# Prompt attention of a hybrid encoder step: the two maps of a differential head joined before the values product

## The reference

```python
logits = jnp.einsum('bqhcd,blhcd->bhcql', qb, kb).astype(f32) * (DH_B ** -0.5)
logits = logits - _alibi_slopes(H_B)[None, :, None, None, None] * dist
logits = jnp.where(adm, logits, -jnp.inf)
p = jax.nn.softmax(logits, axis=-1)
a = (p[:, :, 0] - lam * p[:, :, 1]).astype(vb.dtype)
return jnp.einsum('bhql,blhe->bqhe', a, vb)
```

## Time and profile before

| | us |
|---|---|
| median of 3 runs | 4177.35 (4172.96 to 4182.59) |
| the profiled execution | 4171.43 |
| its span, first to last instruction | 4169.9 |
| prompt attention in it, first logits to last output | 1378.2 |
| mean granted TensorE clock | 0.94 |

### The profile page before, as it was taken

How to read it: one execution, slowest core, us unless ns; L and a number is a source line. 1 busy time by engine, 2 the same in 40 slices (tenths; PEclk the granted TensorE clock), 3 DMA queues, 4 the chain that set the end, 5 groups by cost and what they waited for, 6 DMA issues and landing times. The chain is left out here.

```text
span 4169.9 us, 56226 instructions
## 1 busy us (share of the span) xinstructions
PE 3748.4 (90%) x20713; PEld 3178.6 (76%) x20713; DVE 2326.8 (56%) x4784; ACT 1676.0 (40%) x2562; POOL 186.8 (4%) x373
## 2 busy tenths in 40 slices
PE   8989996884788988888988799999999999989997
PEld 6877883443677878888987678877888788779996
DVE  4335651444788888888775344445445444544334
ACT  2223431112566767777875422232323232322221
POOL 0001110000000000000000010001000100010000
PEclk9999995996799999999999899999999999999998
DMA  5556435627322121111100132223223322322121
GB/s 156 156 153 207 158 131 170 201 69 194 74 50 55 40 51 35 35 36 37 26 16 16 52 131 86 105 101 131 101 101 111 111 102 99 126 96 80 61 79 46
DMA packets 279876, 394.51 MB, mean 95 GB/s; under 512 B 29584, under 2 KB 181136, under 8 KB 270864
## 3 DMA queue, kind: packets, MB, share of 16 engines
q1 hardware_dynamic: 244208, 336.77, 25.9%
q0 software_dynamic: 12160, 44.18, 3.3%
q10 hardware_dynamic: 23328, 11.22, 1.1%
HBM read 320.32 MB, written 71.80 MB: 94 GB/s over the span
## 5 line engine op out<-in xcount | busy, mean ns | idle before, releaser
L1138 PE MATMUL pPV<-pV,pPTr 128*128 128x128 f32 (+1 forms) x4864 | 651.4, 282 | 36.8 <-ACT pPTr L1202 21.4
L1138 PEld LDWEIGHTS pPV<-pV,pPTr 128*128 128x128 f32 x4864 | 613.8, 198 | 57.6 <-issue 15.7
L1202 ACT ACTIVATE pPTr<-pTP 128x512 f32<-128x512 f32 (+3 forms) x704 | 355.7, 535 | 284.2 <-PE pTP L1125 281.5
L2167 ACT ACTIVATE fRU<-fUP 128x512 f32<-128x512 f32 (+1 forms) x128 | 80.0, 625 | 930.6 <-PE fUP L2037 930.6
L2037 PE MATMUL fUP<-fA_hi,fW_hi 128*128 128x512 f32 (+1 forms) x1280 | 418.9, 360 | 20.0 <-DVE fA_lo L2209 20.0
L2037 PE MATMUL fDN<-fW_hi,fU_hi 128*128 128x512 f32 x1088 | 423.6, 389 | 2.1 <-DVE fY L2307 2.1
L2037 PE MATMUL fDN<-fW_lo,fU_hi 128*128 128x512 f32 x1088 | 423.4, 389 | 0.0
L2037 PE MATMUL fDN<-fW_hi,fU_lo 128*128 128x512 f32 x1088 | 423.2, 389 | 0.0
L2037 PE MATMUL fUP<-fA_lo,fW_hi 128*128 128x512 f32 (+1 forms) x1280 | 418.3, 359 | 0.0
L2037 PE MATMUL fUP<-fA_hi,fW_lo 128*128 128x512 f32 (+1 forms) x1280 | 417.8, 359 | 0.0
L2203 DVE TENSOR_TENSOR fW_lo<-fW_raw,fW_hi 128x2048 fp32r<-128x2048 f32 x144 | 333.3, 2336 | 129.6 <-ACT fW_hi L2122 129.6
(11 more groups left out here) (237 smaller groups left out, 6254.2 us busy)
## 6 DMA issues: line engine op xcount, KB each, us to landing
fW_raw<-w_up SPq DMA_DIRECT2D x64, 1024.0 KB, 5.0
fW_raw<-w_down SPq DMA_DIRECT2D x64, 1024.0 KB, 4.9
qT<-qOUT SPq DMA_DIRECT2D x40, 512.0 KB, 3.3
sKB<-cache_kb SPq DMA_DIRECT2D x8, 2048.0 KB, 14.0
sVB<-cache_vb SPq DMA_DIRECT2D x8, 2048.0 KB, 8.4
pQA<-qT SPq DMA_DIRECT2D x64, 256.0 KB, 4.9
pQB<-qT SPq DMA_DIRECT2D x64, 256.0 KB, 5.0
fW_raw<-w_o SPq DMA_DIRECT2D x16, 1024.0 KB, 5.5
```

The costliest lines, as they stand in the source:

```text
L1138: mm = pe.matmul(PV[g % 2][:, 0:size], PTr[n % 3][:, j - 4 * k, :], V[:, j, a:a + size], start=(j == 0), stop=(j == blk[t] - 1))
L1202: act.activation(PTr[n % 3][:, 0:size, :], TP[bank_use[("p", n)] % 2][:, 0:size, :], ACT.Copy).then_inc(s_pt, 1)
L2167: act.activation(RU[:, 0:nt * P].rearrange("p (n w) -> p n w", n=n), UP[f % 2][:, 0:n, 0:width], ACT.Relu).then_inc(s_ru, 1)
```

## The change

The two maps of a B head are joined before the values. When both rows of exp are there, DVE computes a coefficient c = sum0 * (-lambda) / sum1 and, in one pass over the n keys, X1 = X1 * c + X0. Only the joined row, that of the odd job, is transposed and multiplied with V; its output is scaled with 1/sum0. So each head has one apply instead of two, and OM's and the lambda product's small steps go.

Around it: X has three buffers; PE makes logits three jobs ahead, the first half early in a job and the rest late; ACT's exp runs two jobs ahead; DVE's round g takes the pass of job g + 2, and inverts two sums at once in every even round. The fused pass multiplies by -slope and takes the minimum, so that the minimum itself is the bias of exp (scale -1), and the bias product goes. The selection is laid out anew: one ACT count in every job 0 to 12, five DVE steps in each of the rounds 1 to 12, and all that remains (two small steps and the mask passes) in round 13, where before it was spread up to round 15. The lambdas are loaded into OT's memory, and a third X buffer is zeroed at the start.

```diff
+    XB, AHEAD = 3, 3
+    def applied(g):
+        return g % JOBS < H_A or g % 2 == 1
...
             def select_steps(m):
-            last = count(HALVINGS)
+            last = HALVINGS // 2
             if m == 0:
-                return (0, 0), (0, 0)
...
+                return 0, 1
+            if m <= last:
+                return count(2 * m - 2) + 1, count(2 * m)
+            if m == last + 1:
+                return count(2 * m - 2) + 1, SEL
+            return SEL, SEL
...
         def _(pe):
-                early = g + 2 < NG and groups[t] > 1
+                early = g + AHEAD < NG and groups[t] > 1
                 transposes(0)
                 for k in range(1, groups[t]):
                     transposes(k)
                     if k == 1 and early:
-                        queries_keys(g + 2, slice(0, 2))
+                        logits(g + AHEAD, slice(0, 1))
                     products(k - 1)
-                if g + 2 < NG:
-                    queries_keys(g + 2, slice(2, None) if early else slice(None))
+                if g + AHEAD < NG:
+                    logits(g + AHEAD, slice(1, None) if early else slice(None))
                 products(groups[t] - 1)
...
-                apply(g)
+                if applied(g):
+                    apply(g)
+                elif g + AHEAD < NG:
+                    logits(g + AHEAD)
...
         def _(act):
             def softmax(g):
-                act.wait_ge(s_nm, g + 1)
-                act.activation(X[g % 2][:, 0:n_of[t]], X[g % 2][:, 0:n_of[t]], ACT.Exp,
-                               bias=nm[:, g % 2:g % 2 + 1], scale=slope,
+                act.wait_ge(s_lx, halves_before(g + 1))
...
+                act.activation(X[g % XB][:, 0:n_of[t]], X[g % XB][:, 0:n_of[t]], ACT.Exp,
+                               bias=mx[:, g % 4, k:k + 1], scale=-1.0,
...
-                for k in range(groups[t]):
-                    if k == 2 and g + 1 < NG:
-                        softmax(g + 1)
+                for k in range(groups[t] if applied(g) else 0):
+                    if k == 2 and g + 2 < NG:
+                        softmax(g + 2)
...
         def _(dve):
-                if g >= 2:
-                    dve.wait_ge(s_tr, groups_before(g - 1))
+                if g >= XB:
+                    if applied(g - XB):
+                        dve.wait_ge(s_tr, groups_before(g - XB + 1))
+                    else:
+                        dve.wait_ge(s_cb, combined_before(g - XB + 1))
...
-                                             scale=1.0, scalar=mx[:, i, k - 1:k] if k else -3.0e38,
-                                             op0=ALU.add, op1=ALU.max, accum_out=mx[:, i, k:k + 1])\
+                                             scale=-SLOPE[m], scalar=mx[:, i, k - 1:k] if k else 3.0e38,
+                                             op0=ALU.add, op1=ALU.min, accum_out=mx[:, i, k:k + 1])\
...
+            def combine(g):
+                n = n_of[g // JOBS]
+                i, j = g % 4, combined_before(g)
+                c = cf[:, j % 2:j % 2 + 1]
+                dve.wait_ge(s_ri, g // 2 + 1)
+                dve.tensor_scalar(c, sm[:, i:i + 1], lv[:, 5:6], ri[:, i + 1:i + 2], ALU.mult, ALU.mult)\
+                    .then_inc(s_cf, 1)
+                dve.wait_ge(s_cf, j + 1)
+                x = X[(g + 1) % XB][:, 0:n]
+                dve.scalar_tensor_tensor(x, x, c, X[g % XB][:, 0:n], ALU.mult, ALU.add).then_inc(s_cb, 1)
...
             for g in range(NG):
                 t, m = divmod(g, JOBS)
+                if g + 2 < NG:
+                    take(g + 2)
+                if m % 2 == 0:
+                    invert_sums(g)
+                    if m >= H_A:
+                        combine(g)
+                if g > 0 and applied(g - 1):
                     output(g - 1)
```

More of the change, by code:

```diff
@@ L869, in attend_prompt @@
     NG = PT * JOBS
+    SLOPE = SLOPE_A + [s for s in SLOPE_B for _ in range(2)]
+    def applied(g):
+        return g % JOBS < H_A or g % 2 == 1
     sems = []
@@ L887, in attend_prompt @@
         DT = sb("DT", [P, PKEYS])
-        X = [sb(f"X{i}", [P, XW]) for i in range(2)]
+        X = [sb(f"X{i}", [P, XW]) for i in range(XB)]
         junk = sb("junk", [P, PKEYS], mybir.dt.int8)
@@ L944, in groups_before, with outputs_before, combined_before @@
         def groups_before(g):
-            return sum(groups[i // JOBS] for i in range(g))
+            return sum(groups[i // JOBS] for i in range(g) if applied(i))
+        def outputs_before(g):
+            return sum(1 for i in range(g) if applied(i))
+        def combined_before(g):
+            return sum(1 for i in range(g) if not applied(i))
         def bank_users():
[L950 to L954, removed]
+            banks, bank_use = [], {}
             def bank(kind, n, free):
@@ L958, in bank @@
                 banks.append(free)
-            for g in range(-2, NG):
-                if g + 2 < NG:
[L962 to L968, removed]
+            for g in range(NG):
+                t, m = divmod(g, JOBS)
+                if m == 2 and t > 0:
+                    for k in range(2 * t - 2, 2 * t):
+                        bank("f", k, (s_fc, k + 1))
+                if applied(g):
+                    for k in range(groups[t]):
                         bank("p", groups_before(g) + k, (s_pt, groups_before(g) + k + 1))
@@ L1073, in _ @@
             pe.wait_ge(s_c, 80)
[L1074 to L1082 removed]
+            used = {"banks": 0}
             def free_bank():
@@ L1089, in free_bank, with logits @@
                 return TP[u % 2]
-            def logits(t, q, km, signal, some=slice(None)):
-                for a in range(0, n_of[t], L)[some]:
-                    dst = free_half()
-                    for b in range(a, min(a + L, n_of[t]), 512):
-                        size = min(512, n_of[t] - b)
-                        for u in range(2):
-                            mm = pe.matmul(dst[:, b - a:b - a + size], q[:, u, :], K[:, km, b:b + size],
-                                           start=(u == 0), stop=(u == 1))
-                    mm.then_inc(signal, 1)
-            def queries_keys(g, some=slice(None)):
+            def logits(g, some=slice(None)):
                 t, m = divmod(g, JOBS)
@@ L1162, in finish @@
                     tr.then_inc(s_ft, 1)
-            queries_keys(0)
-            queries_keys(1)
+            for g in range(AHEAD):
+                logits(g)
             for g in range(NG):
@@ L1203, in take @@
                                    ACT.Copy).then_inc(s_pt, 1)
-                if groups[t] <= 2 and g + 1 < NG:
-                    softmax(g + 1)
+                if (groups[t] <= 2 or not applied(g)) and g + 2 < NG:
+                    softmax(g + 2)
             def finish(t):
@@ L1229, in _ @@
             dve.wait_ge(s_c, 80)
-            dve.memset(X[0][:, :], 0.0).then_inc(s_x0, 1)
-            dve.memset(X[1][:, :], 0.0).then_inc(s_x0, 1)
+            for i in range(XB):
+                dve.memset(X[i][:, :], 0.0).then_inc(s_x0, 1)
             for i in range(2):
```

174 lines of the change are left out of this document (73 added, 101 removed).

## The result

The changed kernel takes 4198.97 us (median; 4196.41 to 4210.09) against 4177.66 of the kernel before on the same chip: the ratio is 1.0055, with a 95% interval of 1.0042 to 1.0067. It is slower, by 21 us; the prediction had said 18 us faster. The profiled execution took 4200.5 us, its span 4199.0.

A forecast was written before the change was run, and what follows sets the result against it. The prediction took PE and DVE as co-bound, with time to gain where the pipe drains and refills between tiles. Terms +24+14-38-4-15 = -19 us, rounded to -18, took 4177 to 4159 us; range 4112 to 4200.

The forecast's parts named there:

- I take 2.4 GHz: PE in the new pairs: despite one gap near 3.5 us per pair, the clock stays at full speed.
- (b): Dense pairs (8,9) and (10,11) of tiles 1 to 14: +24 us.
- DVE's part: DVE's added and removed passes: a new pair takes 12.4 us against 11.8 before in tile 11.
- (d): A jobs: unchanged from tile 7 on, where PE-bound; some 0.1 us each less up to tile 6, -4 us.
- (e): Tile 15, without selection: a pair takes some 13.8 us instead of 17.1; with the drain -15 us.
- clock rival: Pairs run at 1.2 GHz: about 2 us on 16 dense pairs of tiles 7 to 14, +32, 4191 us; chance 0.10.
- (c): From the pass of job 14 to the end of the selection: 0.2 to 1.5 us per tile, +14 us.
- (a): Refill, from selection end to the next tile's dense pace: shorter, -6.0 us in tile 11, -38 us in all.
- DVE over 90% occupied in tiles 5 to 14: Sign that the prediction is right: DVE's occupancy in those tiles exceeds 90%.
- Refill not shortened: Rival: slowly restarted PE makes DVE wait as long as before between tiles; +20, 4197 us; chance 0.20.
- Moves with no price: Earlier query requests, exp two jobs ahead and a late sign count on ACT: no cost counted.
- PE is the bound: Rival: all 191 us of PE's removed work come off the time, 3986 us; chance 0.05.

The follow-up runs named there:

- e1: Changed kernel plus twelve unread identity matmuls in PE's idle gap in the joined pairs (8,9) and (10,11) of tiles 7 to 14; 4176.15 us.
- e9: The kernel of e4 plus the same twelve matmuls in jobs 9 and 11 of tiles 7 to 14, where PE has no gap; 4196.05 us.
- e10: The kernel of e6 plus 21 to 52 unread identity matmuls in PE's gap at job 14 of tiles 1 to 13; 4126.91 us.
- e4: Changed kernel without the join: each map has its own transposes, copies and products, the deeper pipeline stays; 4150.70 us.
- e7: Changed kernel with only pairs (12,13) and (14,15) of each tile joined, the others applied map by map; 10.5 us over e6.
- e3: Changed kernel with the join pass over 16 columns only, the rest of that computation left out, waits and order as before; 4123.62 us.
- e2: Changed kernel with PE's products of joined rows ahead of logits, and ACT's copies ahead of sign count and exp; 43 us slower than the changed kernel.
- e6: Changed kernel with only the last pair of each tile joined, the other three pairs applied map by map; 4137.21 us.

## Why the prediction was wrong

**The step that failed is "I take 2.4 GHz"** in the part on the clock. It had the pattern right, PE working 7.7 of 12.4 us in a pair with one gap near 3.5 (3.0 measured in tile 11), and read the clock off tile 2's jobs, where the row showed 1.00. The pairs ran at 0.85, 0.88 and 0.80 in tiles 8, 11 and 14. Filling the gaps gave back 21.6 us of (b) and 22.8 us of the kernel (e1), the same filling without a gap cost 42 (e9). With that term (b) would have been 24+21.6 = 45.6, measured 42.7; the sum of DVE's part, +24, was good, as e1's +21.1 shows. But this step is 19 of the 40 us between the forecast sum and the measured one; (d) is 14 and (e) 9.5 (the other three places add up to -2). With the clock kept, e1 stands at 4176 us and not at 4159, so the clock alone doesn't account for the missing gain.

The rule set beside it (the Trainium skill, TensorE: Matmul & The Clock Gate, Why this matters for your kernels), no idle gaps between bursts, was the better guide; the trace agrees, with 3 us of idle and a logits matmul of 0.5 instead of 0.22 us behind it. It isn't the whole of it, as the 2.83 us gap of e3 with a clock of 1.00 behind it shows. The clock rival built on it had chance 0.10 and +32 us for the 16 pairs, since it took the lower clock for the whole pair; the rows show it mainly in the odd rounds (tile 11: 0.73 in both, 1.00 in the even ones), and the cost there is 1.3 us a round.

**(d), forecast -4, measured +9.8.** "Here the deeper pipe hides nothing that costs." +5.2 of it is tile 2 and +4.0 tile 4. Jobs 5 to 9 of tile 2, before and then in the changed kernel:

```profile
1113.80:1127.00 13.20, 10.04 (x78) 8.52 (x78) 11.66 (x57) 9.72 (x25) 0.00 (x0) 1.00 0.42 80
```

```profile
1110.50:1128.80 18.30, 17.52 (x71) 15.02 (x72) 11.15 (x47) 10.08 (x27) 0.00 (x0) 0.50 0.40 86
```

The clock stayed at half throughout. Every run with the new pipeline loses 4.6 to 5.2 us in these jobs of tile 2, the one without a join too, so that isn't the join's. Why the clock doesn't come back there wasn't settled, and e10, with the refill filled, has it too. The 4.0 us of tile 4 move from trace to trace: tile 4 has 0.1 in e4 and 0.4 in e10, while tile 3, 0.8 here, has 6.2 in e7 and 7.1 in e10, with a clock of 0.51 in its jobs. So column (d) of two runs can differ by several us with no cause in the edit.

**(e), forecast -15, measured -5.5.** Two pairs of tile 15 are 15.2 and 15.7 us instead of 13.8, where 17.1 stood. The first of them by rounds, even and odd:

```profile
2338.10:2344.50 6.40, 4.31 (x24) 3.29 (x22) 5.59 (x10) 2.39 (x3) 0.00 (x0) 1.00 0.00 0
2344.50:2353.30 8.80, 7.52 (x49) 7.20 (x50) 2.76 (x7) 4.38 (x6) 0.00 (x0) 0.81 0.00 0
```

The estimate followed DVE's path and let PE keep up; in the odd round PE is busy 7.52 of 8.80 us, at a clock of 0.81. With the join of the last pair the drain is 2.3 us longer. Without the long join (e3) a pair is 12.1 us, its odd round 7.62 at a clock of 1.00, and the stretch with its drain is -16.7; the estimate less its 2.13 us for the columns left out would be 11.7. So the path was nearly right without the join, and is 1.4 to 1.9 us a pair too short with it. How much of that is the clock and how much the join on PE's path wasn't separated.

**What held.** The join is 1.84 us at 1552 keys and 2.37 at 2064, the even round 7.4 us, (c) +14.8 for +14, and (a) -37.5 for -38, though -47.7 by the prediction's own cut at the fifth pass. A jobs of tile 11 stayed at 5.8 us. The refill behind tile 11, first pass of tile 12 to its fifth, is 22.3 us where 28.0 stood, forecast 22.0. Of the signs, PE idle for microseconds in every pair came, and DVE over 90% occupied in tiles 5 to 14 didn't: it is 82 to 88%, pass to pass. "Refill not shortened", 0.20 and 4197 us, gave nearly the measured time for a reason that did not occur: the refill did shorten.

**"Moves with no price".** The prediction said that in pairs one of two jobs has no copies, "which covers" a late sign count on ACT. The count does wait 3.54 us and does hold the copies back, but e1's odd round of 5.2 us leaves at most 0.3 us for it beside DVE's own 4.9. Where the order was changed to help (e2), it cost a microsecond a round.

**PE is the bound**, 0.05 and 3986 us: 104 us came off PE's busy time and the kernel got slower. In e4 PE is as busy as it was before and the kernel is 26 us faster. Busy time is no bound by itself.

What stays open: why tile 2 runs at half clock in each version with the new pipeline, and how much of e4's 26 us is due to the third buffer, the logits three jobs ahead, the bias or the order of the selection, each alone. Variants with two buffers, or with the logits two jobs ahead, weren't tried: the order of the queues would have to change with them. The profiled span behind the stage's last output is 7.4 us longer in the changed kernel, in code that the change doesn't touch; the same code takes 1798.2 to 1802.5 us in the ten runs, 1799.0 before and 1806.4 in the changed kernel, so part of it at least is scatter between executions.

## What to carry to other kernels

When two engines are both nearly full in the dense part, moving work from one to the other costs a good part of its duration (38 us of joins cost the pairs 21 with the clock kept), and leaves gaps on the relieved one, which cost another 22 here: check the granted clock there before calling the relief free. The same move pays in the drain and refill of the pipe, where only one of the two is waited for, so apply it to those rounds alone (e6: 13.5 us, against a loss of 48 when it was applied everywhere). And test the deeper pipeline and the algebraic change in separate kernels first: here one was worth 26 us and hid how much the other lost.

## What was unexpected of the hardware

- A gap of 3.0 us on PE between bursts was followed by a granted clock of 0.74 over the next 6.5 us, at 1.2 GHz by the doubled durations, while the 7.4 us in which the gap began ran at 1.00. A gap of 2.83 us in e3 was followed by 1.00, and one of 2.91 by 0.75. Twelve 128x128 f32 matmuls (2.84 us) in the gap kept it at 1.00.
- GpSimd takes 7.66 us for a multiply and an add over 128x1552 f32, for which DVE's one fused pass takes 1.84. While it runs, a 128x1 SCALAR_TENSOR_TENSOR on DVE took 3.13 and 2.22 us instead of 0.22, and over the stage 62 of 86 that began during such a pass took longer; a DVE count over 1680 columns beside it was not slower.
